# Norm sums of q and k as two f32r passes, and the stores of the last convolution rows between two loops of weight loads

## The reference

```python
h = swiglu_half(h, *ffn1)                   # first feed-forward, 22 tiles of 128
p = rmsnorm(h, norm_g) @ w_in               # -> q | k | v | z | beta | alpha | glu
qkv = silu(causal_dwconv(qkv_ext, qkv_conv_w))
q = l2norm(q) * DK ** -0.5; k = l2norm(k)   # x * rsqrt(sum(x * x) + EPS), 4 heads of 128
o, s = gated_delta_chunked(q, k, v, g, beta, s0, chunk)
o = rmsnorm(o, o_norm_g) * silu(z)
c_in = val * sigmoid(gate)
c_ext = concatenate([s_conv, c_in])
new_s_conv = c_ext[:, -(CONV_WIDTH - 1):]   # the last 30 rows go back to memory
c = silu(rmsnorm(causal_dwconv(c_ext, conv_w) + conv_b, conv_norm_g))
h = h + concatenate([o, c]) @ w_out
h = swiglu_half(h, *ffn2); y = rmsnorm(h, final_norm)
```

## Time and profile before

| | us |
|---|---|
| median of 3 runs (1204.36 to 1205.02) | 1204.9 |
| the profiled execution | 1204.62 |
| its span, first to last instruction | 1202.6 |
| PE busy | 1190.0 (99%) |
| DVE busy | 788.3 (66%) |
| ACT busy | 515.5 (43%) |
| norm sums, start of the first to start of what follows the last | 590.3 to 619.8 |
| the eight stores of `last_c`, issue of the first to landing of the last | 586.7 to 607.7 |

### The profile page before, as it was taken

The page is one execution under the profiler, slowest core; times in us unless marked ns, Lnnn a source line. Parts: engine busy times, 40 slices in busy tenths (PEclk is TensorE's granted clock), DMA queues, the critical chain, the costliest instruction groups (busy, mean ns, idle before and its releaser), DMA issues.

```text
span 1202.6 us, 21067 instructions
## 1 busy us (share of the span) xinstructions
PE 1190.0 (99%) x8832; PEld 1162.1 (97%) x8832; DVE 788.3 (66%) x1155; ACT 515.5 (43%) x820; POOL 76.5 (6%) x58
## 2 busy tenths in 40 slices
PE   9999999999999999999999999999999999999997
PEld 9999999999999998999989898999999999999997
DVE  6887565767566633766557787547776667675764
ACT  6345343435344532433443444443344344353355
POOL 0000000000000300000125210220000000000003
PEclk9999999999999999999999999999999999999999
DMA  5321212221212422211510002422133121222112
GB/s 191 128 87 72 105 62 97 89 105 71 106 71 105 117 95 70 67 57 54 122 9 1 1 2 88 132 70 89 53 116 124 69 97 63 97 106 105 71 71 79
DMA packets 39212, 99.68 MB, mean 83 GB/s; under 512 B 12112, under 2 KB 15568, under 8 KB 39120
## 3 DMA queue, kind: packets, MB, share of 16 engines
q1 hardware_dynamic: 38064, 96.00, 23.4%
q10 hardware_dynamic: 1056, 2.36, 0.5%
HBM read 92.91 MB, written 5.44 MB: 82 GB/s over the span
## 4 chain that ended last, share of the span: by engine, by line
PE 92%; issue 3%; DVE 2%; ACT 1%; POOL 1%; DMA 0%; POOLq 0%; DVEq 0%; SPq 0%
PE ps L846 34%; PE ps L813 21%; PE ps L762 19%; PE ps L958 10%; PE ps L1349 4%; PE ps L726 1%; PE ps L1155 1%; PE ps L1363 1%; ACT x_hi L1431 1%; DVE w_lo L1926 1%; DVE h L1988 1%; PE ps L928 0%; PE ps L982 0%; PE ps L1261 0%; DMA h<-x_t 0%
## 5 line engine op out<-in xcount | busy, mean ns | idle before, releaser
L846 PE MATMUL ps<-x_hi,s_hi 128*128 128x296 f32 (+1 forms) x576 | 171.2, 297 | 0.2
L846 PE MATMUL ps<-x_hi,s_lo 128*128 128x296 f32 (+1 forms) x576 | 170.9, 297 | 0.0
L846 PE MATMUL ps<-x_lo,s_hi 128*128 128x296 f32 (+1 forms) x576 | 170.9, 297 | 0.0
L762 PE MATMUL ps<-x_hi,w_hi 128*128 128x296 f32 (+1 forms) x608 | 136.1, 305 | 0.3 <-DVE x_lo L1931 0.3
L762 PE MATMUL ps<-x_lo,w_hi 128*128 128x296 f32 (+1 forms) x608 | 131.8, 298 | 0.0
L762 PE MATMUL ps<-x_hi,w_lo 128*128 128x296 f32 (+1 forms) x608 | 131.7, 298 | 0.0
L846 PE MATMUL ps<-t_hi,s_hi 128*128 128x296 f32 (+1 forms) x432 | 128.3, 297 | 0.0
L846 PE MATMUL ps<-t_hi,s_lo 128*128 128x296 f32 (+1 forms) x432 | 128.1, 297 | 0.0
L846 PE MATMUL ps<-t_lo,s_hi 128*128 128x296 f32 (+1 forms) x432 | 128.0, 296 | 0.0
L2025 DVE TENSOR_TENSOR s_lo<-s_sum,s_hi 128x1024 fp32r<-128x1024 f32 x72 | 88.2, 1225 | 43.0 <-ACT s_hi L1418 40.3
L846 PEld LDWEIGHTS ps<-x_hi,s_hi 128*128 128x128 f32 x576 | 108.4, 188 | 0.6 <-issue 0.6
(11 more groups left out here) (322 smaller groups left out, 2556.4 us busy)
## 6 DMA issues: line engine op xcount, KB each, us to landing
raw<-weights SPq DMA_DIRECT2D x150, 512.0 KB, 3.3
raw<-weights SPq DMA_DIRECT2D x16, 384.0 KB, 3.5
S<-states SPq DMA_DIRECT2D x1, 2048.0 KB, 11.8
new_state<-S ACTq DMA_DIRECT2D x1, 2048.0 KB, 6.9
y_t<-h SPq DMA_DIRECT2D x4, 336.0 KB, 2.3
h<-x_t SPq DMA_DIRECT2D x4, 296.0 KB, 5.0
h<-x_t SPq DMA_DIRECT2D x2, 592.0 KB, 7.0
raw<-weights SPq DMA_DIRECT2D x4, 256.0 KB, 5.3
```

The lines of the kernel that those rows point to most:

```text
L762: last = nc.tensor.matmul(ps[:, slot if out is None else out, half, 0:w_half], w[:, slot, k, :], x[:, k, a:a + w_half], start=(k == 0 and ...
L846: last = nc.tensor.matmul(out, w[:, k, :], x[:, k, :], start=(start and k == 0 and r == 0), stop=(k == KT // 2 - 1 and r == 2), skip_group ...
```

## The change

**Norm sums.** Behind the two squares ACT casts both (640 or 1024 columns) into a new tile `norm_hi`, and DVE subtracts into `norm_lo` (`norm_rest`), which lies in the place of `work`. `norm_sums` then makes four f32r matmuls per tile, high and low part of q and of k, in place of two in f32. `norm_hi` lies in memory that `c_ext` also covers; therefore ACT waits before the first cast until the stores of `last_c` have landed (`c_stored`) and the last window of the convolution has been read (`win_ps`). `norm_sums` waits for `qk_sq_lo` in place of `qk_sq`.

**Stores.** The eight stores of `last_c`, with their wait for `c_in_ready`, go from behind the load of `S` to the place between the loop that ends with unit `U_QKV + 3` and the loop that begins with `U_QKV + 4`.

Two pairs of semaphores are merged (`dft_in` with `state_in`, `wba_hi_ready` with `wba_ready`), with the counts waited for raised to match.

```diff
-            with sp.Fori(0, (U_OUT + 2 - U_QKV - 4) // 2) as i:
-                load_pair(2 * i + U_QKV + 4)
-            sp.wait_ge(conv_ps, NBLK)
-            sp.wait_ge(unit_done, U_GLU)
-            sp.dma_start(S[:, :, 1:NG, :], states).then_inc(state_in, 16)
             sp.wait_ge(c_in_ready, NC_)
             for c in range(NC_):
                 sp.dma_start(last_c[:, c, 0:30], c_ext[:, c, L:L + 30]).then_inc(c_stored, 16)
                 sp.dma_start(last_c[:, c, 30:270].rearrange("p (b w) -> p b w", b=NB),
                              c_ext[:, c, CP:CE].rearrange("p (b w) -> p b w", b=NB)[:, :, LB:CS]).then_inc(c_stored, 16)
+            with sp.Fori(0, (U_OUT + 2 - U_QKV - 4) // 2) as i:
+                load_pair(2 * i + U_QKV + 4)
+            sp.wait_ge(conv_ps, NBLK)
+            sp.wait_ge(unit_done, U_GLU)
+            sp.dma_start(S[:, :, 1:NG, :], states).then_inc(tables_in, 16)
             sp.wait_ge(lastq_saved, NQ)
...
-                pe.wait_ge(s["qk_sq"], t + 1)
+                pe.wait_ge(s["qk_sq_lo"], t + 1)
...
-                mm(heads(b0, n), ones[:], h4(work[:, 2 * (t % 2), :], n))
-                mm(heads(b1, n), ones[:], h4(work[:, 2 * (t % 2) + 1, :], n)).then_inc(s["norms_ps"], 1)
+                for q, b in enumerate((b0, b1)):
+                    for part in (norm_hi, norm_lo):
+                        last = mm(heads(b, n), ones[:].bitcast(F32R), h4(part[:, 2 * (t % 2) + q, :], n),
+                                  start=part is norm_hi, stop=part is norm_lo)
+                last.then_inc(s["norms_ps"], 1)
...
                 nc.scalar.activation(h4(work[:, 2 * p + 1, :], n), kv[:, 0:H, cols], ACT.Square).then_inc(s["qk_sq"], 1)
+                act.wait_ge(s["qk_sq"], t + 1)
+                if t == 0:
+                    act.wait_ge(c_stored, 16 * 2 * NC_)
+                    act.wait_ge(win_ps, NBLK)
+                both_of = slice(2 * p, 2 * p + 2), slice(0, H * n)
+                nc.scalar.copy(norm_hi[:, both_of[0], both_of[1]], work[:, both_of[0], both_of[1]]).then_inc(s["qk_sq_hi"], 1)
...
+            def norm_rest(t):
+                n, p = TILES[t][1], t % 2
+                both_of = slice(2 * p, 2 * p + 2), slice(0, H * n)
+                dve.wait_ge(s["qk_sq_hi"], t + 1)
+                V.tensor_tensor(norm_lo[:, both_of[0], both_of[1]], work[:, both_of[0], both_of[1]],
+                                norm_hi[:, both_of[0], both_of[1]].bitcast(F32), ALU.subtract).then_inc(s["qk_sq_lo"], 1)
```

More of the change, by code:

```diff
@@ L337, in build @@
         overlay = ExitStack()
-        sb("work_head", [P, 4, QW], F32, overlay)
+        norm_lo = sb("norm_lo", [P, 4, QW], F32R, overlay)
         xoc_lo = sb("xoc_lo", [P, NC_, QW], F32R, overlay)
@@ L369, in build @@
         overlay = ExitStack()
+        norm_hi = sb("norm_hi", [P, 4, H * P], F32R, overlay)
+        overlay.close()
         xoc_hi = sb("xoc_hi", [P, NC_, TOK], F32R, overlay)
@@ L521, in build @@
         psum_free = sem("psum_free")
-        x_in = [sem(f"x_in{q}") for q in range(len(X_PIECES))]; vec_in = sem("vec_in"); norm_in = sem("norm_in"); hist_in = sem("hist_in"); state_in = sem("state_in")
+        x_in = [sem(f"x_in{q}") for q in range(len(X_PIECES))]; vec_in = sem("vec_in"); norm_in = sem("norm_in"); hist_in = sem("hist_in")
         ones_set = sem("ones_set")
@@ L533, in build @@
         g_hi_ready = sem("g_hi_ready"); g_ready = sem("g_ready")
-        wba_hi_ready = sem("wba_hi_ready"); wba_ready = sem("wba_ready")
+        wba_ready = sem("wba_ready")
         pads_set = sem("pads_set")
@@ L539, in build @@
         sig_ready = sem("sig_ready"); c_in_ready = sem("c_in_ready")
-        dft_in = sem("dft_in"); taps_ps = sem("taps_ps"); taps_ready = sem("taps_ready")
+        tables_in = sem("tables_in"); taps_ps = sem("taps_ps"); taps_ready = sem("taps_ready")
         win_ps = sem("win_ps"); win_ready = sem("win_ready"); spec_ps = sem("spec_ps"); spec_ready = sem("spec_ready")
@@ L921, in gate_products @@
             def gate_products():
-                pe.wait_ge(wba_ready, 1)
+                pe.wait_ge(wba_ready, 2)
                 pe.wait_ge(rstd_ready, 2)
@@ L966, in tap_transform @@
                 if q == 0:
-                    pe.wait_ge(dft_in, 16)
+                    pe.wait_ge(tables_in, 16)
                     pe.wait_ge(psum_free, U_QKV)
@@ L1272, in state_heads @@
                 if hd == 0:
-                    pe.wait_ge(state_in, 16)
+                    pe.wait_ge(tables_in, 32)
                     pe.wait_ge(s["ek_ready"], 1)
@@ L1594, in _ @@
             nc.scalar.activation(expa[:], v("a_log", 0, H), ACT.Exp)
-            nc.scalar.copy(wba[:, :, 0:2 * H], v("w_ba", 0, KT * 2 * H).rearrange("p (k c) -> p k c", k=KT)).then_inc(wba_hi_ready, 1)
+            nc.scalar.copy(wba[:, :, 0:2 * H], v("w_ba", 0, KT * 2 * H).rearrange("p (k c) -> p k c", k=KT)).then_inc(wba_ready, 1)
             root(0)
@@ L2208, in _ @@
                 add_square(k)
-            dve.wait_ge(wba_hi_ready, 1)
+            dve.wait_ge(wba_ready, 1)
             V.tensor_tensor(wba[:, :, 2 * H:], v("w_ba", 0, KT * 2 * H).rearrange("p (k c) -> p k c", k=KT),
@@ L2364, in tok @@
                                 ALU.mult).then_inc(s["tok_ready"], 1)
+            def norm_rest(t):
[4 more added lines that the diff above has]
+                                norm_hi[:, both_of[0], both_of[1]].bitcast(F32), ALU.subtract).then_inc(s["qk_sq_lo"], 1)
+            norm_rest(0)
             dve.wait_ge(conv_ps, NBLK)
+            norm_rest(1)
             z_scaled(0)
@@ L2372, in _ @@
             z_scaled(1)
+            norm_rest(2)
             qk_scaled(1)
             z_scaled(2)
+            norm_rest(3)
             qk_scaled(2)
@@ L2377, in _ @@
             z_scaled(3)
+            norm_rest(4)
             dve.wait_ge(unit_done, U_OUT)
```

4 lines of the change are left out of this document (2 added, 2 removed).

## The result

| | before | after |
|---|---|---|
| median of 12 runs each | 1204.89 us (1204.36 to 1208.02) | 1209.01 us (1207.40 to 1212.03) |
| profiled execution, its time / its span | 1204.62 / 1202.6 us | 1209.86 / 1207.7 us |
| mean granted clock of the span | 0.997 | 0.994 |

The changed kernel takes 1.0032 times as long, with a 95% interval of 1.0020 to 1.0044: slower, by 4.1 us. The forecast was 1208.8. That is 0.3%, the difference of two larger parts, as the trace shows.

The account below looks back on a forecast made before the run. PE, busy 99% of the span, was taken to bound the kernel. 1204.62 - 2.5 (sums) + 5.1 (stall) + 1.3 (slow clock) = 1208.5, with the median 0.28 higher: 1208.8 us, range 1203.5 to 1211.5.

Parts of the forecast that it names:

- Part 1: Norm sums on PE: f32r matmuls save 3.7 us, reduced to 2.5 by a wait at tile 4.
- PE's wait at tile 4: Between the sums of tiles 3 and 4, PE waits 1.2 us for tile 4's low part.
- Part 2: New casts on ACT and subtractions on DVE: no wait on PE except for tile 4's low part.
- Part 3: Stores ahead of U_QKV + 4's load: late weights hold ACT's cast and tap copies; PE stalls 5.1 us before window_in(0).
- the landing of the load: U_QKV + 4's weights, queued behind the eight stores, land at 490, between 489.6 and 491.1.
- The edge of the cover: Ahead of window_in(0): 3.3 us of cover, so the price is the load's landing minus 484.9.
- rival E: Delta stage's slow clock stretch comes twice, or load later than 492: 1212 us and over; chance 0.04 shared with another rival.
- the duration of 13.7 us: Time taken for the eight stores' 4608 packets of 120 bytes to move, from the kernel before.
- rival C: Stores much quicker with nothing preceding them in the queue, load lands before 484.9, sums' gain kept: 1202.4 us; chance 0.16.
- Part 4: Granted clock falls to half near 490.6, after PE's stall before window_in(0), costing 1.3 us.
- the row of the tail: At the kernel's end the clock fell to half 2.6 us after PE's last matmul; a 5.1 us stall is longer.
- The sum: Whole kernel: profiled 1204.62 - 2.5 + 5.1 + 1.3 = 1208.5, with the median 0.28 higher: 1208.8 us.

Follow-up runs that it names:

- e3: Changed kernel with loads of U_QKV + 4 and + 5 ahead of the stores, plus tile 4's subtraction ahead of the emptying of U_Z + 3: 1201.93 us.
- e8: Kernel before, f32 sums kept, with the stores put behind the loads of U_QKV + 4 and + 5: 1204.25 us.
- e1: Changed kernel with the loads of U_QKV + 4 and + 5 put back ahead of the eight stores: 1200.42 us.
- e6: Changed kernel with the four large stores read as 240 neighbouring floats, pieces of 960 bytes instead of 120, so stored rows hold other values: 1200.35 us.
- e2: Kernel before, f32 sums kept, with only the eight stores moved ahead of the load of U_QKV + 4: 1213.97 us.
- e7: Changed kernel with the stores of two channels ahead of the loads of U_QKV + 4 and + 5 and two behind: 1202.16 us.
- e2's twin: Kernel before with only the eight stores moved ahead of the load of U_QKV + 4, run once more on another chip: 1212.35 us.
- e4: Changed kernel with ACT's four tap copies put ahead of its cast of U_QKV + 4: 1204.93 us.
- e5: Changed kernel with 38 additional matmuls, results unread, in PE's idle time ahead of window_in(0): 1208.00 us.
- e10: Changed kernel run once more, unaltered, on another chip: 1210.60 us.

## Why the prediction was right

**What bounds the kernel.** Right: PE has 99% of the span, and the stall came through at full length in the milestones. Not every wait does: taking away the 1.1 us at tile 4 (e3) brought PE only 0.3.

**Part 1, the sums.** 0.91 us a tile was forecast, 0.93 measured; 2.5 us in all, against 2.3 by the milestones and 2.5 by e8 against e1 and e6. Right, with the reduction by PE's wait at tile 4 (1.2 forecast, 1.1 measured). Without it the forecast of this part would have been 3.7.

**Part 2, free four times of five.** Right: norm_lo of tile 4 is the only one that PE waits for. That the wait guards little was not foreseen: with it gone (e3) PE waits 0.7 us for ACT's gate factors.

**Part 3, the stores.** Right in each step of the path: the load behind the stores, ACT at the cast, the tap copies, window_in(0). The step that was off is the landing of the load: 490 was forecast, 491.2 measured. The last store was put at 489.6 and came at 489.8; the load's own move behind it was taken at 0.4 us, out of 0 to 1.5, and was 1.4. So the term was 6.4 (window_in(0), 494.36 - 487.97; e2's stall is 6.3) where 5.1 was forecast. The edge of the cover, 484.9, agrees with e7. In the last set, on another chip, the stall was 8.1 in the changed kernel, above the range of 0 to 7 given for it, and 7.0 in e2's twin. The stores' drain is not one number: from the issue of the first to the landing of the last it took 15.2 to 15.9 us in the four traces of the changed order in the sets before (after, e2, e4, e5) and 15.8 to 17.1 in the four of the last set (last landing at 478.51 + 13.4 = 491.9 in e10). There the changed kernel was 6.0 us over the one before, not 4.1, with the load at 493.2, later than the 492 of rival E, and yet at 1210.6 and not at that rival's 1212.

That the duration of 13.7 us was right is in part luck. It was taken from stores that had queued behind 2 MB, as one duration for the whole; here they took 489.8 - 475.9 = 13.9, the sum of a burst (1182 and 919 packets in two microseconds), as rival C would have it, a slower rest up to 486, and some 4 us in which hardly any small packet moves and the landing is still out. The picture of a queue in which the stores drain until 489.6 and only then the load moves was wrong in the same place: the load's first packets moved at 483. Rival C was wrong on what comes behind the burst, not on the burst.

**Part 4, the clock.** A fall was forecast and came, for 1.3 us of loss; 1.5 are lost between the milestones, 1.0 to 1.9 by filling the stall. The instant was not near 490.6 but at 494.3, 4.7 us after PE's last matmul of 489.65; in e10 it was at about 490.3, 2.0 us after that of 488.3, and in e2 at 492.9, 5.0 us after that of 487.9. So the row of the tail, 2.6 us, gives an order of size and no date. (A granted clock of 0.95 over 1198 to 1199 puts the tail's fall at 1198.9, not at 1198.95; the 2.6 stays.) That the size came out near is luck: 1.3 was the middle between two lengths of a stretch begun in the stall, while the real one, of 3.4 us, lay whole in PE's work.

The Trainium skill (TensorE: Matmul & The Clock Gate, HAM oscillation) says that waits for DMA between bursts of matmuls bring the array back to the slow clock; all five executions with an unfilled stall agree, with 0.50 behind it, and the two with a filled one, with 1.00.

**The sum.** Against the profiled execution of before the terms gave +3.9 (-2.5 + 5.1 + 1.3); the two profiled executions are 5.2 apart (-2.3 + 6.4 + 1.5 - 0.5, and 0.1 outside the span). So the sum was 1.3 short of the trace, nearly all of it the landing of the load. That the medians are only 4.1 apart, and the forecast 0.2 from the result, is because the profiled execution of after lies 0.85 above its median, while that of before lies 0.27 below its own. The forecast hit the median closer than its terms deserve.

## What to carry to other kernels

Before a store is moved ahead of a load in the same queue, count its contiguous pieces, not its bytes, and count them on the side that is cut finer: 4608 pieces of 120 bytes delayed the load by over 9 us, and the same bytes, with all but 512 of the pieces joined into ones of 960, by nothing that PE felt. Find the slack of the load from the consumer backwards (cast, copies, matmul), and put between loads only what fits in it. Here the two loads first and then the stores, with the f32r sums kept (e1), is the version that beats both kernels: 1200.42 us, 0.9970 of before [0.9961, 0.9979]. Leaving the stores where they were is no way to it, by an estimate from the kernel before: they landed there at 607.7, and the first cast, which now has to wait for them, has to be ready for a sum at 590.3. No run has this order.

## What the runs showed of the hardware that I had not expected

- Small pieces have more than one rate in one queue: about 900 to 1200 of 120 bytes in each of the first two full microseconds, then 320 to 430, then 230 to 290. And a load of large packets behind 2304 of them is slow as well (e7, 0.07 to 0.12 MB a microsecond for four microseconds). The pieces are taken sooner than they are finished, out of sight of the packets' own times: a store whose packets had been moved by 480 landed at 484.4 (e7), one whose packets had been moved by 487 at 489.8 (the changed kernel), while in e6 all landed within 2.0 us of their issue. What holds the landing back stays open.
- One kernel on one chip has times in steps rather than a spread: e1 at 1200.3, 1202 and 1203.5, e8 at 1202.8 and 1204.5, each step with a lower mean granted clock. The traces show one stretch of about 3.4 us at half clock more or less, worth 1.5 to 2 us, mostly between 630 and 645 us, where PE has short work with short waits; in e5 it was at about 743 to 746. What decides whether it comes was not settled. A change worth under 2 us needs to be read at the same step: e1 and e8 differ by 2.5 there, and by 3.8 in their medians.
- The clock's fall keeps no fixed distance from PE's last matmul: 2.0 us (e10), 4.7 (the changed kernel) and 5.0 (e2) in stalls of the same kind. A wait of 1.6 us (e4) had no fall behind it.
- Such a stretch is free when it falls ahead of a wait: the one at 480.7 to 484.1 in the changed kernel only made the stall shorter.
